# Dense expert weights of a product-key expert layer: one-hot products on TensorE against adding indirect transfers in DRAM

## What is computed

```python
def _peer(h, w_q, k1, k2, u, vt):
    q = (h @ w_q).reshape(B, S, PEER_HEADS, 2, PEER_HALF)
    s1 = jnp.einsum('bshd,hnd->bshn', q[..., 0, :], k1)
    s2 = jnp.einsum('bshd,hnd->bshn', q[..., 1, :], k2)
    v1, i1 = lax.top_k(s1, PEER_TOPK)
    v2, i2 = lax.top_k(s2, PEER_TOPK)
    cand = (v1[..., :, None] + v2[..., None, :]).reshape(B, S, PEER_HEADS, PEER_TOPK * PEER_TOPK)
    vs, ic = lax.top_k(cand, PEER_TOPK)
    e = (take(i1, ic // PEER_TOPK) * PEER_N_KEYS + take(i2, ic % PEER_TOPK))
    w = jax.nn.softmax(vs, axis=-1)
    act = jax.nn.gelu(einsum('thkd,td->thk', u[e], hx)) * w
    return einsum('thk,thkd->td', act, vt[e])
```

## Time and profile before

| | |
|---|---|
| median of 3 executions | 3407.71 us (3404.61 to 3408.12) |
| profiled execution, first to last instruction | 3407.6 us |
| PE busy | 3368.6 us, 99% of the span |
| DVE busy | 2274.0 us, 67% |
| ACT busy | 1409.9 us, 41% |
| POOL busy | 634.2 us, 19% |
| mean granted TensorE clock | 0.997 of full speed |
| DMA | 797.53 MB, mean 234 GB/s |

### The profile page before, as it was taken

How to read it: one execution, slowest core, us unless ns; L and a number is a source line. 1 busy time by engine, 2 the same in 40 slices (tenths; PEclk the granted TensorE clock), 3 DMA queues, 4 the chain that set the end, 5 groups by cost and what they waited for, 6 DMA issues and landing times.

```text
span 3407.6 us, 42319 instructions
## 1 busy us (share of the span) xinstructions
PE 3368.6 (99%) x15582; PEld 2797.0 (82%) x15582; DVE 2274.0 (67%) x2275; ACT 1409.9 (41%) x1125; POOL 634.2 (19%) x342
## 2 busy tenths in 40 slices
PE   9999999999999999999999999999999999999998
PEld 7888888888888888888888888888888888888886
DVE  7664545788888888856676493555557776765556
ACT  6333343343333333343554334444443333333333
POOL 0000003300000000100000188777730000000000
PEclk9999999999999999999999999999999999999999
DMA  7555556788888888744454456767776666656552
GB/s 273 189 189 186 188 197 237 307 309 308 319 325 301 307 316 326 265 173 173 161 202 181 167 215 218 247 238 245 243 270 234 231 221 240 234 200 222 201 205 99
DMA packets 151463, 797.53 MB, mean 234 GB/s; under 512 B 15284, under 2 KB 48356, under 8 KB 64192
## 3 DMA queue, kind: packets, MB, share of 16 engines
q1 hardware_dynamic: 85168, 610.47, 48.9%
q0 software_dynamic: 27216, 149.96, 11.9%
q10 hardware_dynamic: 38976, 35.66, 3.3%
HBM read 756.09 MB, written 39.91 MB: 234 GB/s over the span
## 4 chain that ended last, share of the span: by engine, by line
PE 92%; DVE 4%; DMA 1%; ACT 1%; issue 1%; POOL 0%; ACTq 0%; DVEq 0%; SPq 0%; POOLq 0%
PE ps L1961 29%; PE ps L1963 29%; PE ps L1962 29%; PE ps L1993 2%; PE ps L2480 1%; ACT hi L576 1%; DMA adaraw<-in_w_ada 1%; DVE lo L1094 1%; DVE adaacc L1391 1%; PE ps L2110 0%; PE ps L2087 0%; DMA w_scratch<-wst 0%; PE ps L2098 0%; PE ps L2420 0%; DMA wc<-w_scratch 0%
## 5 line engine op out<-in xcount | busy, mean ns | idle before, releaser
L576 ACT CAST hi<-raw 128x2048 fp32r<-128x2048 f32 x576 | 1100.1, 1911 | 1759.0 <-PE ps L1963 1739.0
L1094 DVE TENSOR_TENSOR lo<-raw,hi 128x2048 fp32r<-128x2048 f32 x468 | 1070.9, 2291 | 630.8 <-ACT hi L576 618.2
L1961 PE MATMUL ps<-hi,hTh 128*128 128x512 f32 x3040 | 1197.0, 394 | 1.7 <-DVE hTl L1162 1.1
L1962 PE MATMUL ps<-lo,hTh 128*128 128x512 f32 x3040 | 1184.4, 390 | 0.0
L1963 PE MATMUL ps<-hi,hTl 128*128 128x512 f32 x3040 | 1184.1, 389 | 0.0
L1963 PEld LDWEIGHTS ps<-hi,hTl 128*128 128x128 f32 x3040 | 570.8, 188 | 120.4
L1961 PEld LDWEIGHTS ps<-hi,hTh 128*128 128x128 f32 x3040 | 571.4, 188 | 117.4 <-DVE hTl L1162 1.4
L1962 PEld LDWEIGHTS ps<-lo,hTh 128*128 128x128 f32 x3040 | 571.6, 188 | 113.0
L414 POOL TENSOR_TENSOR lo<-raw,hi 128x2048 fp32r<-128x2048 f32 x108 | 500.3, 4635 | 226.3 <-ACT hi L576 226.3
L1961 PE MATMUL ps<-hi,pactTh 128*128 128x512 f32 x992 | 388.2, 391 | 0.0
L1963 PE MATMUL ps<-hi,pactTl 128*128 128x512 f32 x992 | 386.3, 389 | 0.0
(11 more groups left out here) (382 smaller groups left out, 2414.2 us busy)
## 6 DMA issues: line engine op xcount, KB each, us to landing
raw<-in_w_peer SPq DMA_DIRECT2D x256, 1024.0 KB, 4.9
raw<-in_w_ffn SPq DMA_DIRECT2D x132, 1024.0 KB, 6.4
adaraw<-in_w_ada POOLq DMA_DIRECT2D x96, 1024.0 KB, 6.5
raw<-in_w_first SPq DMA_DIRECT2D x88, 1024.0 KB, 4.8
raw<-in_w_second SPq DMA_DIRECT2D x72, 1024.0 KB, 4.8
raw<-in_w_merge SPq DMA_DIRECT2D x28, 1024.0 KB, 6.6
w_scratch<-wst ACTq DMA_DIRECT2D x64, 256.0 KB, 5.4
wc<-w_scratch POOLq DMA_DIRECT2D x32, 512.0 KB, 5.2
```

Source lines behind the costliest of these rows:

```text
L576: nc.scalar.copy(hi[:, s, :], raw[:, s, :]).then_inc(hi_done, 1)
L1094: V.tensor_tensor(lo[:, s, :], raw[:, s, :], hi[:, s, :].bitcast(F32), ALU.subtract).then_inc(lo_done, 1)
L1961: T.matmul(out, th[stat], hi[:, s, cut], start=start, stop=False)
L1962: T.matmul(out, th[stat], lo[:, s, cut], start=False, stop=False)
```

## The change

The dense weights are no longer products of one-hot rows. POOL clears `w_d` with 16 transfers of 1 MB from a tile of zeros, paced by the pieces of the second block's input projection. DVE works out for each pick the index of its cell in `w_d` (row of the token times 16384, plus first key times 128, plus second key) while it would wait for ACT's exponentials. Once the picks' weights are there, POOL issues 256 indirect transfers: each takes one weight from each of 128 partitions (4 bytes) and adds it to the cell whose index stands in `cell`. For each head and each half of the tokens there are 16; a head's transfers of one half wait until those of the head before, of the same half, have landed. The 64 batches of one-hot rows, products, copies, sums and stores go, and so do the six transposes of the picks. The rests of groups 8 to 24 are DVE's; POOL keeps those of groups 1 to 7. `load_group(0, 0)` and `load_group(1, 1)` now wait for the adding transfers. EARLY stays 25.

```diff
@@ POOL, during the second block's input projection
+            nc.gpsimd.memset(zeros[:], 0.0).then_inc(sem("zeros"), 1)
+            pool.wait_ge(sem("zeros"), 1)
+            def clear_weights(first, last):
+                for i in range(first, last):
+                    pool.wait_ge(piece_used, 4 * Q_IN2 + 3 * i // 2)
+                    part = w_d[16 * i:16 * i + 16].rearrange("t (a n) -> (t a) n", n=2048)
+                    pool.dma_start(part, zeros[:]).then_inc(sem("w_zero"), 16)
+            clear_weights(0, 6)
             pool.wait_ge(sem("cum"), 2)
             load_sums(0)
+            clear_weights(6, 13)
             pool.wait_ge(sem("scores2"), 4)
             load_sums(1)
+            clear_weights(13, 16)
@@ POOL, expert layer
-            with pool.Fori(0, EARLY - 2) as g:
+            with pool.Fori(0, EARLY_TOP - 1) as g:
                 for s in range(4):
                     rest_piece(g + (Q_PEER + 1), s)
+            def add_picks(h, k):
+                pool.wait_ge(sem(f"w_add{k}"), 16 * TOPK * h)
+                for n in range(TOPK):
+                    to = bass.IndirectOffsetOnAxis(ap=cell[:, k, h, n:n + 1], axis=0)
+                    nc.gpsimd.indirect_dma_start(out=w_cells, out_offset=to, in_=picks[:, k, 2, h, n:n + 1], in_offset=None,
+                                                 compute_op=ALU.add).then_inc(sem(f"w_add{k}"), 16)
+            pool.wait_ge(sem("w_zero"), 16 * 16)
+            pool.wait_ge(sem("places"), 1)
+            pool.wait_ge(sem("picks"), 1)
+            for h in range(8):
+                for k in range(TOK):
+                    add_picks(h, k)
...
+            for k in range(TOK):
+                pool.wait_ge(sem(f"w_add{k}"), 16 * TOPK * 8)
             pool.wait_ge(sem("hid_st"), 16 * 2)
-            pool.wait_ge(sem("one_hots"), 1)
-            load_hidden(0, 0)
-            load_hidden(1, 1)
-            for s in range(4):
-                rest_piece(Q_PEER + EARLY - 1, s)
-            for u in range(2):
-                pool.wait_ge(sem(f"w_st{u}"), 16 * (SEQ // 8))
-            load_group(0, 0, hidden=False)
-            load_group(1, 1, hidden=False)
+            load_group(0, 0)
+            load_group(1, 1)
@@ ACT: weights_out, store_weights and weights_by are gone
-                early_group(EARLY_TOP + u, u, lambda s: weights_by(4 * u + s, s % 2))
+                early_group(EARLY_TOP + u, u, lambda s: None)
@@ DVE, between the exponents' input and their use
+            step(V.tensor_tensor(work[:, 0, 0:P], ident[:], iota[:], ALU.mult))
+            step(V.tensor_reduce(row0[:], work[:, 0, 0:P], AX.X, ALU.add))
+            step(V.tensor_scalar(row0[:], row0[:], float(EXPERTS), None, ALU.mult))
+            for k in range(TOK):
+                ins = V.scalar_tensor_tensor(picks[:, k, 0], picks[:, k, 0], float(N_KEYS), picks[:, k, 1], ALU.mult, ALU.add)
+            step(ins)
+            for k in range(TOK):
+                ins = V.tensor_scalar(cell[:, k], picks[:, k, 0], row0[:, 0:1], float(P * k * EXPERTS), ALU.add, ALU.add)
+            ins.then_inc(sem("places"), 1)
@@ DVE, behind the choice: one_hots and weights_sum are gone
+            V.memset(y[:], 0.0).then_inc(sem("y_sum"), 2)
+            dve.wait_ge(lo_done, 4 * (Q_PEER + EARLY_TOP))
+            with dve.Fori(Q_PEER + EARLY_TOP, Q_PEER + EARLY) as q:
+                for s in range(4):
+                    rest_piece(q, s)
@@ PE
-            early_group(EARLY_TOP - 1, 1, choice_turn)
+            early_group(EARLY_TOP - 1, 1)
-                early_group(EARLY_TOP + u, u, lambda s: expert_weights(4 * u + s, s % 2))
+                early_group(EARLY_TOP + u, u)
```

More of the change, by code:

```diff
@@ L154 @@
     "wexp_in": "DVE: chosen scores less their maximum", "wexp": "ACT: exponentials", "picks": "DVE: choice and weights",
[L155 to L159, removed]
+    "zeros": "Pool: a row of zeros", "w_zero": "DMA: dense weights cleared in DRAM", "places": "DVE: picks' places in the dense weights",
+    "w_add0": "DMA: picks of the first 128 tokens added to the dense weights", "w_add1": "DMA: those of the others",
     "gelu": "ACT: groups' hidden values", "hid_st": "DMA: early groups' in DRAM", "hid_in0": "DMA: back, even groups",
@@ L265, in program @@
     gacc = at("gacc", [P, TOK, 512], F32, A + 53 * K)
[L266 to L269, removed]
+    cell = at("cell", [P, TOK, 8, TOPK], U32, A + 51 * K)
+    zeros = at("zeros", [P, 2048], F32, XO + 8 * K)
     y = at("y", [P, TOK, D], F32, A)
@@ L987, in _ @@
             early_group(EARLY_TOP - 1, 1, lambda s: None)
[L989 to L1005, removed]
             for u in range(2):
-                early_group(EARLY_TOP + u, u, lambda s: weights_by(4 * u + s, s % 2))
+                early_group(EARLY_TOP + u, u, lambda s: None)
             with act.Fori(EARLY_TOP // 2 + 1, (EARLY - 1) // 2) as m:
                 for u in range(2):
-                    early_group(2 * m + u, u, lambda s: weights_by(8 * m + (4 * u + s - 4 * EARLY_TOP), s % 2))
-            store_weights(SEQ // 4 - 1, 1)
+                    early_group(2 * m + u, u, lambda s: None)
             def peer_hi(b, u):
@@ L1781, in _ @@
             ins.then_inc(sem("picks"), 1)
[L1782 to L1796, removed]
-                rest = rests[:, tok].rearrange("p (t o) -> p t o", o=1).to_broadcast([P, 4, P])
-                V.tensor_tensor(oh2[:, v, :, 0], row, second, ALU.is_equal)
-                V.tensor_tensor(oh1[:, v], row, first, ALU.is_equal).then_inc(sem("one_hots_raw"), 1)
-                dve.wait_ge(sem("one_hots_raw"), n + 1)
-                chosen = oh2[:, v, :, 0].bitcast(F32)
-                V.tensor_tensor(oh2[:, v, :, 1], chosen, rest, ALU.mult).then_inc(sem("one_hots_lo"), 1)
-                dve.wait_ge(sem("one_hots_lo"), n + 1)
-                V.tensor_tensor(oh2[:, v, :, 0], chosen, weight, ALU.mult).then_inc(sem("one_hots"), 1)
@@ L1806, in weights_sum @@
-            def weights_sum(n, v):
-                dve.wait_ge(sem("weights_out"), n + 1)
-                V.tensor_tensor(wst[:, v], wst[:, v], weight_parts[:, :, 1], ALU.add).then_inc(sem("w_sum"), 1)
-            one_hots(0, 0)
-            one_hots(1, 1)
-            weights_sum(0, 0)
-            with dve.Fori(1, SEQ // 8) as i:
-                for v in range(2):
-                    one_hots(2 * i + v, v)
-                    weights_sum(2 * i + (v - 1), 1 - v)
-            weights_sum(SEQ // 4 - 1, 1)
+            dve.wait_ge(sem("sc_out"), 4)
@@ L2457, in _ @@
                     early_group(2 * m + u, u)
[L2459 to L2482 removed]
+            early_group(EARLY_TOP - 2, 0)
+            early_group(EARLY_TOP - 1, 1)
             for u in range(2):
[L2485 removed]
+                early_group(EARLY_TOP + u, u)
             with pe.Fori(EARLY_TOP // 2 + 1, (EARLY - 1) // 2) as m:
                 for u in range(2):
[L2488 removed]
+                    early_group(2 * m + u, u)
             def peer_turn(b):
@@ L2495, in first_turn @@
                 if s == 2:
-                    pe.wait_ge(sem("w_sum"), SEQ // 4)
                     peer_turn(0)
```

25 lines of the change are left out of this document (3 added, 22 removed).

## The result

| | before | changed |
|---|---|---|
| median | 3407.91 us (3404.61 to 3410.04, 4 executions) | 3601.6 us (3599.92 to 3603.74, 4 executions) |
| ratio | 1 | 1.0569, 95% interval 1.0554 to 1.0584 |
| profiled execution, first to last instruction | 3407.6 us | 3600.2 us |
| mean granted TensorE clock | 0.997 | 0.966 |

The change makes the kernel 193.7 us slower. The forecast was 3372.8 us, and the range ended at 3520.

What follows compares the result with a forecast made beforehand. PE was taken to bound the kernel: 32.0 us of batches, 0.6 of transposes and 2.2 of wait leave it, all else hidden, so 3407.6 - 34.8 = 3372.8 us. Its own range was 3368 to 3378, the 8-in-10 range up to 3520.

Steps and rivals of the forecast that it cites:

- What bounds the kernel: PE, busy for 99% of the span: what leaves its queue leaves the time until another engine is late.
- What leaves PE: 64 batches 32.0 us, six transposes 0.6 us, wait at the first weights turn 2.2 us: 34.8 us less.
- DVE's new rests and the hand-over: DVE's rests, groups 8 to 24: ready 2.3 us earlier; taking turns delays by at most 4.6 us, hidden.
- The cell indices: Seven small DVE instructions within its 23.77 us idle for ACT's exponentials, below 16 us: nothing is paid.
- The clearing: 16 transfers of 1 MB in the input projection, 301 GB/s in sum: cost 0, with 2 us for the range.
- The adding transfers: POOL's 256 transfers at 1.17 us each (modT row), hidden before PE's first turn; up to 1.43 us fits; chance 0.60.
- rival 2: Each index or addition handled one after the other: 4.6 us a transfer, +777 us, 4185 us; any above 2.3; chance 0.10.
- The formula itself: For transfers too slow to hide, time changes by 256 t - 400.6 us, t being POOL's time per transfer.
- The rule that speaks against it: VectorE instructions with two SBUF inputs and GpSimd ones reading SBUF exclude each other; untested for transfers with indices.
- Rival 1: VectorE's rests hold POOL's index-reading transfers: 2.0 us each, +111 us, 3519 us; chance 0.18, together with transfers slow by themselves.
- Rival 3: Just late: transfers between 1.43 and 1.6 us, part of the gain; at 1.5 us, -17 us, 3391 us; chance 0.08.
- Rival 4: Products go but time stays, since another wait takes a batch's place on PE: about 3407 us; chance 0.04.

Runs made afterwards that it cites:

- x2_half: Changed kernel with 128 of the 256 adding transfers (heads 0 to 3): median 3373.56 us, 0.9898 of the kernel before.
- x6_psum_early31: Changed kernel with rests reading one operand from PSUM and 31 instead of 25 early groups, all transfers kept: median 3375.9 us, 0.9908 of the kernel before.
- x3_plain: Changed kernel with transfers that write instead of add: span 3447.3 us.
- x1_no_rests: Changed kernel with VectorE's rests in groups 8 to 24 made of the first 8 of 2048 columns only: span 3483.6 us.
- x4_psum: Changed kernel where, in groups 8 to 24, ScalarE copies rounded pieces to PSUM and VectorE's rests subtract them from there: span 3485.9 us.
- x11_again: x9_plain_psum once more, also timed without a profile: median 3685.23 us of two executions, 1.0813 of the kernel before.
- x7_64: Changed kernel with 64 instead of 128 indices in each of the 256 transfers: span 3582.5 us.
- x9_plain_psum: x4_psum (25 early groups) with transfers that write instead of add: span 3684.5 us.

## Why the prediction was wrong

**What bounds the kernel** was right: PE's queue and the deadline at its first turn. PE started its last product before that turn at 2472.96 us; the forecast had it there at 2473.4.

**What leaves PE** was right: 34.8 us forecast. x2_half, where nothing waits, is 35.6 us under the kernel before in the medians (3409.18 - 3373.56) and 36.8 in the spans; x6_psum_early31, with all transfers, 32.4 in the medians of its own comparison (3408.29 - 3375.9) and 33.6 in the spans.

**DVE's new rests and the hand-over** were right as to DVE and PE: the first rest started at 2094.68 us, none was late. What was missed here is what they do to POOL, below.

**The cell indices** cost nothing, as said: they were done at 2067.5 us, and 17.95 us of the wait for the exponentials were left. The two sums of keys took 4.56 us together, one of them held by POOL's rest, well under the 16 us that the prediction allowed for all seven instructions.

**The clearing** cost nothing: PE was busy for 225.71 of the 230 us of that window, 225.69 before.

**The adding transfers** are the step that failed. "I take the modT row, 1.17 us" was wrong by a factor of two: the mean step was 2.33 us, and so the overlap failed, since the last transfer began 223 us after the 2464.4 us by which it should have landed. The runs take it apart. An issue with indices, alone and plain, is 0.97 us with 0.30 us behind it, 1.27 us (x3_plain): near the row taken, and under 1.43. Adding takes 0.58 us more (x3_plain against x1_no_rests), which made 1.855 us, already above the 1.43 that decide; no row of before held anything like it, and the term of 1.17 us had nothing in it for the adding, which stands only in rival 2. The rests' hold adds 0.46 us in the mean, 0.87 while they run (x1_no_rests, x4_psum). Either cost alone is enough to be late: 1.87 us a step without the hold, 1.72 without adding.

The formula itself came near: 256 x 2.33 - 400.6 = +196 us, against 192.6 in the spans. The turn came 5 us earlier than the formula has it, 3 of them since the transfers began at 2094 us and not at 2097, and the clock, which had no term, took 2.5 back.

Had the term been right, the forecast would still have been in doubt. The only kernel here whose transfers kept near the forecast's pace, 1.27 us, ended them in time and yet took 3685 us (x11_again). Its transfers wrote and did not add; no run shows adding ones at that pace.

**The rule that speaks against it** was weighed too lightly. The issues of w_ada that DVE did not lengthen have no indices, so they said nothing of transfers that read them. The Trainium skill (SBUF — State Buffer, "SBUF: two separate sides") has both conditions that the runs show: two SBUF inputs against a GpSimd instruction that reads SBUF, and a VectorE instruction that uses both ports for one tensor. The trace agrees: 3.28 us beside a rest of two SBUF operands, 2.46 beside a fast copy, 1.55 beside a rest from PSUM (x4_psum).

**Rival 1** had the mechanism, at 0.18, and was off in size. It worked with POOL's share of time, 3.15 of 5.44 us, from a transfer of 1.17 us, and came to 2.0 us and 3519 us. Had it started from 1.855 us, its share would have given 3.2 us beside rests, where 2.72 was measured: a transfer's 0.30 us gap and its first tenth of a microsecond do pass beside a rest, and so does one that is well under way when the rest begins (2109.57 to 2111.12 us, beside the rest of 2110.90). And it took the hold as lasting to the end, though rests stop when PE stands; the last 117 transfers ran alone.

**Rival 2**, each index or addition handled one after the other, is refuted for all 128 in one row: the upper 64 cost 2.3 ns each (x7_64). A price per index in shares that run side by side is not excluded, and what makes up the 0.58 us for adding stays open. The mean step of 2.33 us falls into the stretch that was put under this rival's name, but by other causes. The Trainium skill (GPSIMD Engine Reference, "Performance pitfalls for Q7 kernels") puts a read command per gather index at about 102 cycles. The estimate of 11 us a transfer that the prediction made of it, with one core for all 128, does not fit the 0.97 us measured for a plain one. **Rival 3**, just late, asked for 1.43 to 1.6 us. **Rival 4** did not occur.

The range was too narrow at its upper end because each unknown part of the transfer was bounded as a whole, with 0.28 put on everything above 1.6 us. Two costs of the same sign, adding and holding, both left open, should have carried more. Rival 1's own figure, 3519 us, stood 1 us inside the range's end, so that any larger transfer under the same mechanism fell outside.

## What to carry to other kernels

Work that moves from TensorE to a queue of transfers is worth TensorE's time only if the whole queue fits before its reader: write down the pace per transfer that just fits, and ask of that pace part by part (the issue, the arithmetic in it, what another engine does to it). Here 32768 picks at 128 for each transfer were 256 transfers at 1.855 us, 475 us for a window of 366; in the runs here it took a wider window (31 early groups) as well as a VectorE that reads one operand from PSUM for the 33 us of products to become a gain of 32; either alone left the kernel slower than before (3512 and 3486 us). And before VectorE takes over work from GpSimd, look at whether it then holds what GpSimd does instead. Nor is a faster queue always better: a pace that fits can still stop the others (x9_plain_psum), so time the whole kernel and not the queue alone.

## What the runs showed of the hardware

- A GpSimd transfer with 128 indices occupies it for 0.97 us plain and 1.55 us adding, with 0.30 us to the next; 64 indices on 64 partitions instead of 128 save 0.145 us.
- One that begins beside a VectorE instruction with two operands in SBUF, or beside a copy of 128x2048 in 1.23 us, waits until that ends: 3.28 and 2.46 us. It does not wait for a subtraction of one SBUF and one PSUM operand of 2.29 us. The subtractions kept their 2.29 us in all of these; copies that began while a transfer was under way took up to 1.54 us instead of 1.23.
- Plain transfers of 128 single elements, 1.27 us apart for 330 us, brought all engines nearly to a stop: 20 GB/s, and TensorE with 101 products in 280 us at the lower clock. The same transfers 1.61 us apart in the mean, or adding ones 1.855 us apart, did no harm. What is choked there stays open: the trace puts most of the idle time under "issue", and no run told the cause apart. The DMA engines were busy for 8% in the mean in that window, which speaks against their load. Where between the two paces it sets in was not measured, nor whether it does for other traffic.
- After 225 us without a product TensorE ran at 1.2 GHz, with products 0.43 us apart; this and its return to 2.4 GHz cost 2.5 us.
